# Scoring two 64-wide heads one after the other instead of side by side in a dilated attention

## The reference

```
z = rmsnorm(x) @ w_in ; q, k, v of mixer B: 12 heads of 64, 4 heads for each of three dilations
for (window, dilation) in ((128, 1), (512, 4), (2048, 16)):          # group g = 0, 1, 2
    sc = q k^T / 8 + bias(relative position), outside the band -1e30
    lse = logsumexp(sc) ; o = exp(sc - lse) v
w = softmax over the three groups of lse ; out = sum_g w_g o_g       # 512 x 4 heads x 64
```

## Time and profile before

| | |
|---|---|
| median of 3 runs | 2057.23 us (2055.4 to 2057.28) |
| the profiled execution | 2057.28 us, its span from first to last instruction 2055.4 us |
| mean granted TensorE clock | 0.995 |
| TensorE busy with matmuls | 98% of the span, 9854 matmuls |
| VectorE, ScalarE, GpSimd busy | 55%, 43%, 17% |
| matmuls of `scores_b` | 144, between 35.5 and 125.4 us |

### The profile page before, as it was taken

One profiled execution on the slowest core, in us unless ns is written; L12 is line 12 of the kernel. 1 busy time (PEld: TensorE's weight loads), 2 busy tenths in 40 slices (PEclk: granted clock), 3 DMA queues, 4 the chain that ended last, 5 costly groups with the idle time before them and its releaser, 6 DMA issues.

```text
span 2055.4 us, 25244 instructions
## 1 busy us (share of the span) xinstructions
PE 2023.5 (98%) x9854; PEld 1684.2 (82%) x9854; DVE 1123.9 (55%) x1964; ACT 889.6 (43%) x1750; POOL 344.4 (17%) x337
## 2 busy tenths in 40 slices
PE   8999999999999999999999999999999999999997
PEld 6888778888888888878888888788898888888886
DVE  6767774455434344665443435787775664443434
ACT  5545553345423233553232325777655453322224
POOL 3224330021000001432110101232211021110102
PEclk9999999999999999999999999999999999999999
DMA  5221112243232322233323223223342033233322
GB/s 186 83 73 62 42 43 74 78 158 111 94 101 92 103 92 88 89 103 102 100 94 103 92 82 116 74 73 103 102 140 83 28 116 102 92 95 101 97 87 72
DMA packets 61635, 191.53 MB, mean 93 GB/s; under 512 B 6792, under 2 KB 14472, under 8 KB 61516
## 3 DMA queue, kind: packets, MB, share of 16 engines
q1 hardware_dynamic: 61516, 189.93, 28.7%
HBM read 187.69 MB, written 2.21 MB: 92 GB/s over the span
## 4 chain that ended last, share of the span: by engine, by line
PE 92%; DVE 5%; ACT 1%; DMA 1%; issue 1%; SPq 0%; DVEq 0%; ACTq 0%
PE bank L292 90%; PE bank L297 1%; DVE wl L469 1%; DVE work L190 1%; DVE tmp L181 0%; SPq L169 0%; ACT wh L467 0%; DMA raw<-d_wts 0%; DMA d_tab<-tab_sb 0%; ACT pB L178 0%; ACT rsq L178 0%; DVE x_sb L181 0%; DVE tmp L184 0%; DVE work L181 0%; DVE ssum L181 0%
## 5 line engine op out<-in xcount | busy, mean ns | idle before, releaser
L467 ACT ACTIVATE wh<-raw 128x512 fp32r<-128x512 f32 (+1 forms) x700 | 403.7, 610 | 891.4 <-PE bank L292 887.6
L292 PE MATMUL bank<-h_h,wh 128*128 128x512 f32 x1536 | 609.9, 397 | 7.3 <-ACT wh L467 6.1
L292 PE MATMUL bank<-h_l,wh 128*128 128x512 f32 x1536 | 600.6, 391 | 1.3 <-DVE h_l L184 1.2
L292 PE MATMUL bank<-h_h,wl 128*128 128x512 f32 x1536 | 600.1, 391 | 0.0
L469 DVE TENSOR_TENSOR wl<-raw,wh 128x512 fp32r<-128x512 f32 (+1 forms) x632 | 423.1, 695 | 60.9 <-ACT wh L467 38.8
L292 PEld LDWEIGHTS bank<-h_h,wh 128*128 128x128 f32 x1536 | 289.6, 189 | 71.1 <-ACT wh L467 6.1
L292 PEld LDWEIGHTS bank<-h_l,wh 128*128 128x128 f32 x1536 | 289.8, 189 | 63.5 <-DVE h_l L184 3.7
L292 PEld LDWEIGHTS bank<-h_h,wl 128*128 128x128 f32 x1536 | 289.5, 188 | 61.0 <-DVE wl L469 0.3
L469 POOL TENSOR_TENSOR wl<-raw,wh 128x256 fp32r<-128x256 f32 x134 | 107.1, 826 | 350.5 <-ACT wh L467 350.5
L202 POOL TENSOR_TENSOR tmp<-tmp,rstd 128x512 f32<-128x512 f32 x44 | 63.4, 1442 | 469.4 <-ACT tmp L178 469.4
L181 DVE TENSOR_TENSOR tmp<-bank,rstd 128x512 f32<-128x512 f32 x98 | 70.4, 721 | 115.1 <-PE bank L292 114.5
(11 more groups left out here) (476 smaller groups left out, 3317.0 us busy)
## 6 DMA issues: line engine op xcount, KB each, us to landing
raw<-d_wts SPq DMA_DIRECT2D x314, 512.0 KB, 3.5
raw<-d_wts SPq DMA_DIRECT2D x24, 384.0 KB, 3.0
x_sb<-d_xT SPq DMA_DIRECT2D x16, 256.0 KB, 5.5
raw<-d_wts SPq DMA_DIRECT2D x24, 128.0 KB, 2.0
d_yT<-x_sb SPq DMA_DIRECT2D x4, 384.0 KB, 2.9
tab<-d_ali SPq DMA_DIRECT2D x4, 256.0 KB, 4.3
tab<-d_dec SPq DMA_DIRECT2D x4, 256.0 KB, 3.8
mraw<-d_memT SPq DMA_DIRECT2D x8, 128.0 KB, 2.4
```

Of the source, the lines that this page charges most:

```text
L292: bank.done = pe.add(lambda e: e.matmul(out, lhsT, rhs, start=first, stop=True, skip_group_check=True), n, w, waits)
L467: p.th = [Op(act, lambda e, c=c: e.activation(H[:, c], raw[:, c], FN.Copy), [p.load]) for c in (slice(o, min(o + 512, width)) for o in ran ...
```

## The change

The two heads of a pair are no longer scored together. Before, each of the four steps takes two banks and issues, for each block or class and each of the three products, the matmul of head 0 and right after it the matmul of head 1; the VectorE and ScalarE work of both follows. After, the loop over the heads is outermost: head 0 goes through all four steps, one bank at a time, then head 1. Head 1 also asks for its half of `pB` only when its turn comes. The instructions are the same in kind, shape and number.

```
-        for e in range(2):
-            if p_free[e] is None:
-                yield lambda: p_free[e] is not None
-            was.append(p_free[e])
-            p_free[e] = None
...
-            for x, y, tq, tk in ((q.h, k.h, q.rdy[0], k.rdy[0]), (q.l, k.h, q.rdy[1], None), (q.h, k.l, None, k.rdy[1])):
-                for b, out, hp in zip(bs, outs, heads):
-                    q.free = k.free = [b_mm(b, out, x[hp, lq], y[hp, rk], tq, tk)]
...
-        for g, blks in ((0, (1, 2)), (0, (0, 3)), (1, None), (2, None)):
...
-            for e in range(2):
-                bs.append((yield from bank_of(JOB)))
...
-            for e in range(2):
-                biased(e, bs[e], g, blks)
-            yield
+        for e in range(2):
+            hd, hp = 2 * pr + e, slice(64 * e, 64 * e + 64)
             if p_free[e] is None:
                 yield lambda: p_free[e] is not None
+            was, p_free[e] = p_free[e], None
...
+            def scores(b, out, g, lq, rk):
+                q, k = qk[pr][g]
+                b_mm(b, out, q.h[hp, lq], k.h[hp, rk], q.rdy[0], k.rdy[0])
+                b_mm(b, out, q.l[hp, lq], k.h[hp, rk], q.rdy[1])
+                q.free = k.free = [b_mm(b, out, q.h[hp, lq], k.l[hp, rk], k.rdy[1])]
...
+            for g, blks in ((0, (1, 2)), (0, (0, 3)), (1, None), (2, None)):
+                if not have(*qk[pr][g])():
+                    yield have(*qk[pr][g])
+                yield [t.rdy for t in qk[pr][g]]
+                b = yield from bank_of(JOB)
+                act_table(EXP)
...
+                else:
+                    for c in range(4):
+                        cs = slice(128 * c, 128 * c + 128)
+                        scores(b, b.ap[:, cs], g, cs, cs)
...
+                yield
```

More of the change, by code:

```diff
@@ L1001, in scores_b @@
         last = []
-        heads = slice(0, 64), slice(64, 128)
-        was = []
         for e in range(2):
+            hd, hp = 2 * pr + e, slice(64 * e, 64 * e + 64)
             if p_free[e] is None:
                 yield lambda: p_free[e] is not None
-            was.append(p_free[e])
-            p_free[e] = None
[L1009 to L1013, removed]
-            for x, y, tq, tk in ((q.h, k.h, q.rdy[0], k.rdy[0]), (q.l, k.h, q.rdy[1], None), (q.h, k.l, None, k.rdy[1])):
-                for b, out, hp in zip(bs, outs, heads):
-                    q.free = k.free = [b_mm(b, out, x[hp, lq], y[hp, rk], tq, tk)]
@@ L1018, in exps @@
[L1018 to L1045, removed]
@@ new lines, in scores_b, with exps @@
+            g0, g12 = views_b(e)
+            bias0 = bias_t[0][:, hd * 256:hd * 256 + 256]
+            def scores(b, out, g, lq, rk):
[3 more added lines that the diff above has]
+                q.free = k.free = [b_mm(b, out, q.h[hp, lq], k.l[hp, rk], k.rdy[1])]
+            def exps(g, parts):
+                for s, blk, tk in parts:
+                    tk = a_act(s, s, FN.Exp, tk, bias=nm[:, e, g, blk:blk + 1], accum_out=ss[:, e, g, blk:blk + 1])
+                last.append(tk)
@@ new lines, in scores_b @@
+            for g, blks in ((0, (1, 2)), (0, (0, 3)), (1, None), (2, None)):
[4 more added lines that the diff above has]
+                act_table(EXP)
+                if g == 0:
+                    for n, blk in enumerate(blks):
+                        lo, hi = max(0, 128 * blk - 64), min(S, 128 * blk + 192)
+                        scores(b, b.ap[:, 256 * n:256 * n + hi - lo], 0, slice(128 * blk, 128 * blk + 128), slice(lo, hi))
+                else:
+                    for c in range(4):
+                        cs = slice(128 * c, 128 * c + 128)
+                        scores(b, b.ap[:, cs], g, cs, cs)
+                if blks == (1, 2):
+                    s = b.ap[:, :].rearrange("p (b k) -> p b k", b=2)
+                    t1 = v_tt(g0[:, 1:3, :], s, bias0.unsqueeze(1).to_broadcast([128, 2, 256]), ALU.add, b.done, t_toe, was)
+                    b.free = [t1]
+                    t2 = v_red(nm[:, e, 0, 1:3], g0[:, 1:3, :], ALU.max, t1, negate=True)
+                    exps(0, [(g0[:, 1, :], 1, t2), (g0[:, 2, :], 2, t2)])
+                elif blks == (0, 3):
+                    p0, p3 = g0[:, 0, 64:256], g0[:, 3, 0:192]
+                    t1 = v_tt(p0, b.ap[:, 0:192], bias0[:, 64:256], ALU.add, b.done, t_toe, was)
+                    t2 = v_tt(p3, b.ap[:, 256:448], bias0[:, 0:192], ALU.add, b.done, t_toe, was)
+                    b.free = [t2]
+                    t3 = v_red(nm[:, e, 0, 0:1], p0, ALU.max, t1, negate=True)
+                    t4 = v_red(nm[:, e, 0, 3:4], p3, ALU.max, t2, negate=True)
+                    exps(0, [(p0, 0, t3), (p3, 3, t4)])
+                else:
+                    bt = bias_t[g][:, hd * 128:hd * 128 + 128]
+                    s = b.ap[:, :].rearrange("p (c k) -> p c k", c=4)
+                    t1 = v_tt(g12[g], s, bt.unsqueeze(1).to_broadcast([128, 4, 128]), ALU.add, b.done, t_toe, was)
+                    b.free = [t1]
+                    t2 = v_red(nm[:, e, g, :], g12[g], ALU.max, t1, negate=True)
+                    exps(g, [(g12[g][:, c, :], c, t2) for c in range(4)])
+                yield
```

## The result

The kernel after takes 2069.35 us (median of 4 runs, 2064.98 to 2071.4) against 2056.86 us of the kernel before: +12.5 us by the medians. Nine more executions of it are on record. The median of all thirteen is 2071.25 us, +14.4 us, and the recorded ratio of 1.0066 (interval 1.0051 to 1.0082) amounts to +13.6 us. The forecast was 2063.0 us, +5.7. The direction was right and the size less than half of what came. The median of the four lies just inside the range of 2057 to 2069.5, that of the thirteen outside.

What follows compares the result with a forecast made beforehand. TensorE was taken to bound the kernel, 92% of the chain that ended last. The terms +8.1 + 0.5 - 1.0 - 1.9 = +5.7 us on the profiled 2057.28 us gave 2063.0 us, range 2057 to 2069.5.

Steps and rivals of the forecast that it cites:

- The lost company: Score matmuls on TensorE: a matmul alone on one half costs what a pair costs, +8.1 us.
- The entrances: TensorE's switches between full and half-array matmuls: 8 to 10 stretches instead of seven, +0.5 us.
- The meetings: Where head 0's last step meets head 1's first in TensorE's queue, opposite halves overlap: -1.0 us.
- The waits: TensorE's three pair-0 waits for `qb011` and `qb021` go, with fewer ScalarE exponentials ahead: -1.9 us.
- the sum: The four terms for the change in the scores added together: +5.7 us.
- What moves without a price: Head 1's lumped exponentials delay ScalarE's weight splits, but panels split ahead cover it: no cost, at most 3.4 us.
- three signs: Wrong if lone matmuls stand 0.06 us apart, heads' steps run side by side, or `pa`/`pta_l` waits differ over 3 us.
- The far look ahead: Rival: TensorE reaches far ahead in its queue, so the heads' meeting places return 2.7 us; 2059.9 us, chance 0.11.
- The tail of the mixers: Rival: later queues reorder and mixer A's first stall, 5.3 us, goes; 2057.7 us, chance 0.13.
- All steps apart: Rival: sixteen separate score stretches, no overlap between heads, waits remain; 2068.6 us, chance 0.16 shared with one more stall.

Runs made afterwards that it cites:

- partners with the step later: Kernel after, with unused opposite-half matmuls beside the 144 lone ones and head 0's group-1 step of pair 0 delayed 2.0 us in the plan: 2060.23 us.
- before with the steps later: Kernel before, with pair 0's group-1 step put 1.4 us and group-2 step 0.7 us of planned time later: 2054.03 us.
- Partners: Kernel after, plus 144 matmuls on the opposite half of the array, one behind each lone matmul, results unused: 2066.26 us.
- twelves: Kernel before, with all of head 0's matmuls of a step first, then all of head 1's: 2064.39 us.
- spread: Kernel after, with a pause of 1.3 us of planned time after each step so panel matmuls stand between: 2071.98 us.
- with the step later: Kernel after, with head 0's group-1 step of pair 0 delayed in the plan until TensorE's planned time is 2.0 us further: 2066.58 us.
- threes: Kernel before, with head 0's three products of each block first, then head 1's three: 2056.41 us.

## Why the prediction was too small

*The lost company (+8.1)* was right. The earlier trace rows held: 0.11 us for a lone matmul as for a pair. The cleanest measure is the pair of kernels without low clock between the marks, partners with the step later and before with the steps later. Both have seven stretches, and neither has a return at a meeting. Their marks:

```profile
34.62 0.38 PE L292 MATMUL bank<-qb001h,qb000h 64*128 64x256 f32 x1
188.76 0.39 PE L292 MATMUL bank<-ka_h,qa0h 128*128 128x512 f32 x1
...
34.51 0.39 PE L292 MATMUL bank<-qb001h,qb000h 64*128 64x256 f32 x2
180.54 0.39 PE L292 MATMUL bank<-ka_h,qa0h 128*128 128x512 f32 x1
```

154.14 - 146.03 = 8.1 us, with one wait of 0.3 us left in each. Partners against before, whose waits are alike, is a second reading: 7.9 us. The medians differ by 6.2 us only; the means of the clock, 0.9965 and 0.9956, account for most of the gap.

*The entrances (+0.5)* came to nothing: I expected one to three stretches more, but there are seven in after too, since head 1's four steps all follow head 0's last one. *The meetings (-1.0)* were right in kind and nearly in size. Three matmuls at each are 2 x 3 x 0.112 = 0.7 us, and after is 1.3 us below partners between the marks.

*The waits (-1.9)* failed. I moved ScalarE's work in thought and left the step at its place in the queue. ScalarE did get there earlier, with half the exponentials ahead of it: `qb011h` begins at 43.73 us where it began at 47.03. Its row and that of the matmul that waits for it, in the kernel after (ScalarE's and TensorE's timeline):

```profile
43.73 0.61 ACT L178 ACTIVATE qb011h<-tmp 128x512 fp32r<-128x512 f32 x1
```

```profile
44.40 0.32 PE L292 MATMUL bank<-qb011h,qb010h 64*128 64x128 f32 x1 [1.34 <-ACT qb011h L178]
```

But the planner knew that too and put the step earlier: 27 panel matmuls stand between it and the step before, where there were 42. So TensorE arrived earlier as well. It waits 1.8 us in all against 1.9 for the three waits of before, so this term is 0.0 where the sum had -1.9, and the low window at 45.9 us follows the longer wait. Clock aside, the traces have 6.7 us between the marks where the sum had 5.7: the waits that didn't go and the entrances that didn't come nearly make up the difference.

*What the sum lacked is the clock.* The earlier trace rows were in my hands, low clock behind stalls, and I read them as a price of idle time alone. The two lumps lower it with TensorE busy throughout. In the profiled execution the low windows of the scores are 10.2 us, 6.8 of them behind the lumps. 2.2 us come back behind the second mark, where a low window of mixer A is missing. Over all executions the mean clock gives some 6 us net, against a forecast of none. The step that failed is the sentence that panels cover the lump ("What moves without a price"): it priced the lump on ScalarE only, and TensorE's own clock was never asked for. None of the three signs that I had named for a wrong prediction came, since none of them looks at the clock: the lone matmuls stand 0.11 us apart, head 1's steps are not beside head 0's, and the waits for `pa` and `pta_l` are within 0.5 us.

*The rivals.* The far look ahead fell: twelves shows three matmuls side by side of 12, so whole steps don't come back. The rule that I gave beside it, from the Trainium skill, "TensorE: Matmul & The Clock Gate", section "Part 3: Packing small matmuls — row/col tiling", speaks of weight loads in a window of 64; in this case a matmul of the other half was never seen more than three or four places ahead. The tail of the mixers was reshuffled little: its waits are alike. The low windows of 3.4 and 6.8 us there became one of 3.4 us in the profiled run, which is most of the 2.2 us that it is shorter behind the second mark. "All steps apart" came near the time (2068.6 us) for the wrong reason: the steps stand together, and that is what lowers the clock. When they were set apart, in spread, it was 2072 us.

The low window behind the wait for `qb011h` is of a known kind: the Trainium skill tells in "TensorE: Matmul & The Clock Gate", section "HAM oscillation — how this bites in real kernels", that TensorE, after it has stood waiting in the middle of a kernel, goes on at the lower clock. The trace agrees in kind, with waits of 1.34 and 0.53 us ahead of the window; the example there waits some 3 to 5 us for a transfer. The section does not cover the windows behind the lumps, where TensorE never stood still.

## What to carry to other kernels

Matmuls that contract over 64 partitions should be issued in pairs of opposite halves, at most three of a half in a row: a partner that the kernel needs anyway is free, and it kept the clock up here. Three in a row lost nothing; in twelves, all but three of a head ran alone, with six in a row as with twelve. Before a change puts many half-array matmuls together, ask for the granted clock behind them, not only for their distance. In a kernel whose order comes from a plan, work that gets ready earlier is also placed earlier; a wait goes only if the planned time of the producer is right.

## What the runs showed of the hardware that was not expected

A lump of about 40 matmuls on one half of the array, with no idle time, was followed by 6.8 us at half clock, four times of four (twice in after, twice with the step later); the same lump with partners on the other half kept the clock at 1.00, four times of four. Each of these counts is of one profiled execution per kernel. Three steps of 24 half matmuls in twelves, 18 of them alone (2.4 us), did not lower it. Behind a wait of 1.3 to 2.7 us ahead of half matmuls it was low for 6.8 us in after, spread and twelves, and for 3.4 us with partners. Behind waits of 0.3 and 0.6 us it was low for 3.4 us in threes, and not at all behind 0.59 and 0.63 us in before. Two half streams that are queued one after the other overlap by three matmuls (59.83 beside 60.15; 118.13 beside 118.41), so a matmul of the other half can start ahead of three that stand before it in the queue.
